# First block's norms: the first norm among the first modulation parts, the residual sum ahead of other vector work, first chunks of h marked singly

## What is computed

```python
def modulate(x, gain, shift, scale):
    return rms_norm(x, gain) * (1.0 + scale[:, None]) + shift[:, None]
def swiglu(h, w1, w3, w2):
    return (jax.nn.silu(h @ w1) * (h @ w3)) @ w2
    ...
    cond = jax.nn.silu(c)
    for l in range(DEPTH):
        mod = cond @ ada_w[l] + ada_b[l]
        sh1, sc1, g1, sh2, sc2, g2, sh3, sc3, g3 = jnp.split(mod, N_MOD, axis=-1)
        h = modulate(x, norm_ffn1[l], sh1, sc1)
        x = x + 0.5 * (1.0 + g1)[:, None] * swiglu(h, ffn1_w1[l], ffn1_w3[l], ffn1_w2[l])
        h = modulate(x, norm_mix[l], sh2, sc2)
        y = token_mix(h, ...)
        x = x + (1.0 + g2)[:, None] * y
        h = modulate(x, norm_ffn2[l], sh3, sc3)
        x = x + 0.5 * (1.0 + g3)[:, None] * swiglu(h, ffn2_w1[l], ffn2_w3[l], ffn2_w2[l])
```

## Time and profile before

| | us |
|---|---|
| median of 3 runs | 3086.55 |
| lowest, highest | 3086.18, 3090.66 |
| profiled execution, its own time | 3088.79 |
| its span in the trace | 3086.8 |
| TensorE busy | 2927.2 (95%) |
| VectorE busy | 2096.7 (68%) |
| ACT busy | 1469.9 (48%) |

### The profile page before, as it was taken

The page is one execution under the profiler, slowest core; times in us unless marked ns, Lnnn a source line. Parts: engine busy times, 40 slices in busy tenths (PEclk is TensorE's granted clock), DMA queues, the critical chain, the costliest instruction groups (busy, mean ns, idle before and its releaser), DMA issues.

```text
span 3086.8 us, 53817 instructions
## 1 busy us (share of the span) xinstructions
PE 2927.2 (95%) x22836; PEld 2616.9 (85%) x22836; DVE 2096.7 (68%) x3263; ACT 1469.9 (48%) x1965; POOL 148.2 (5%) x257
## 2 busy tenths in 40 slices
PE   5999999989989998999899999999999999999998
PEld 5888899878878887998788887889788988887887
DVE  5886757768868777566676467755676677556674
ACT  1545644545445364445354345544554345435552
POOL 1000000100000000002000022000100000004000
PEclk6999999999999999999999999999999999999999
DMA  7775326537758743364475533655365555452452
GB/s 248 231 250 162 123 75 208 184 123 241 240 190 264 238 151 99 97 205 151 139 234 167 158 100 110 191 177 164 106 196 184 170 168 183 143 179 83 137 187 99
DMA packets 524878, 521.41 MB, mean 169 GB/s; under 512 B 16615, under 2 KB 521904, under 8 KB 524640
## 3 DMA queue, kind: packets, MB, share of 16 engines
q1 hardware_dynamic: 522032, 517.28, 52.8%
q0 software_dynamic: 816, 0.27, 0.1%
q10 hardware_dynamic: 1792, 0.44, 0.1%
HBM read 516.90 MB, written 1.05 MB: 168 GB/s over the span
## 4 chain that ended last, share of the span: by engine, by line
PE 82%; DVE 9%; ACT 5%; issue 2%; DMA 1%; POOL 0%; SPq 0%; DVEq 0%; POOLq 0%; ACTq 0%
PE P L65 81%; DVE wsp L74 4%; ACT wsp L71 3%; ACT arena L71 1%; DVE ACC L82 1%; PE P L68 1%; DVE arena L74 1%; DVE arena L82 1%; ACT HX L71 1%; DMA raw<-in_ada_w 1%; DVE X L74 1%; ACT L71 0%; DVE HX L82 0%; DVE X L82 0%; DMA raw<-in_nsa_w_in 0%
## 5 line engine op out<-in xcount | busy, mean ns | idle before, releaser
L65 PE MATMUL P<-HX,wsp 128*128 128x512 f32 (+2 forms) x10688 | 1666.2, 318 | 29.8 <-DVE HX L82 18.4
L65 PEld LDWEIGHTS P<-HX,wsp 128*128 128x128 f32 (+1 forms) x10688 | 1505.3, 193 | 169.9 <-issue 21.0
L74 DVE TENSOR_TENSOR wsp<-raw,wsp 128x2048 fp32r<-128x2048 f32 (+3 forms) x448 | 964.6, 2155 | 393.8 <-ACT wsp L71 393.5
L71 ACT ACTIVATE wsp<-raw 128x2048 fp32r<-128x2048 f32 (+3 forms) x448 | 806.0, 1801 | 585.1 <-PE P L65 521.8
L65 PE MATMUL P<-FG,wsp 128*128 128x512 f32 (+1 forms) x2816 | 498.9, 338 | 1.4 <-DVE wsp L74 1.4
L65 PEld LDWEIGHTS P<-FG,wsp 128*128 128x128 f32 x2816 | 429.7, 188 | 65.7 <-DVE wsp L74 2.6
L71 ACT ACTIVATE arena<-P 128x512 f32<-128x512 f32 (+3 forms) x384 | 214.4, 568 | 558.0 <-PE P L65 557.2
L74 DVE TENSOR_TENSOR arena<-arena,P 128x512 f32<-128x512 f32 (+2 forms) x232 | 151.1, 652 | 203.2 <-ACT arena L71 169.7
L65 PE MATMUL P<-arena 64*64 64x64 f32 (+9 forms) x3936 | 244.7, 265 | 21.9 <-ACT arena L71 10.3
L65 PEld LDWEIGHTS P<-arena 64*64 64x64 f32 (+3 forms) x3936 | 195.2, 149 | 68.6 <-issue 33.8
L82 DVE SCALAR_TENSOR_TENSOR ACC<-raw,sm,ACC 128x256 f32<-128x256 f32 x476 | 230.8, 485 | 16.7
(11 more groups left out here) (110 smaller groups left out, 1437.4 us busy)
## 6 DMA issues: line engine op xcount, KB each, us to landing
raw<-in_ffn_w SPq DMA_DIRECT2D x120, 1024.0 KB, 5.3
raw<-in_ada_w SPq DMA_DIRECT2D x72, 1024.0 KB, 5.0
raw<-in_w_in SPq DMA_DIRECT2D x52, 1024.0 KB, 5.2
raw<-in_ffn_w_gate SPq DMA_DIRECT2D x44, 1024.0 KB, 5.3
raw<-in_ffn_w_up SPq DMA_DIRECT2D x44, 1024.0 KB, 5.3
raw<-in_ffn_w_down SPq DMA_DIRECT2D x32, 1024.0 KB, 5.0
raw<-in_ffn_w SPq DMA_DIRECT2D x16, 768.0 KB, 4.6
raw<-in_nsa_w_in SPq DMA_DIRECT2D x12, 1024.0 KB, 5.4
```

Source lines behind the costliest of these rows:

```text
L65: return self if self.e is None else self.e.matmul(*a, skip_group_check=True, **k)
L71: return self if self.e is None else self.e.activation(*a, **k)
L74: return self if self.e is None else self.e.tensor_tensor(*a)
```

## The change

1. Start. The squares, sums, root and reciprocal of norm 0 are moved ahead: on ACT behind the start's copies, on VectorE between the copies of X and its first part, on TensorE the sums stand behind part 0 and the spread behind part 1. `mod_dve` of a part now follows directly, and among the eight parts VectorE and ACT take no FFN weights; behind part 7 ACT splits two units and VectorE one (the low half of the gate weights). The second unit's low half, part 8 and a third unit stand behind the pass over h.
2. Constants. Of 1616 columns the first 256 are loaded first, the others after unit 11; their users wait for the new mark `more_in`.
3. TensorE's products of the parts, all 72, are made in pieces of 64 columns of weights, alternately to partitions 0 to 63 and 64 to 127 of the result, twice as many.
4. Tails of the FFNs and of the output product in the first block. The last additions to X go ahead of the split that stood in front of them, and where the next unit is a part, this part goes behind the pass over h (`ada=False`).
5. Marks. The first pair of chunks of h in the first block has a mark for each chunk (HT, hH and hL). The attention outputs, eight chunks, are waited for one by one in place of pairs.

```diff
         def ready_dve(e, u, last=None, ada=True):
             while made["dve"] <= (reached[u + 1] if last is None else min(last, reached[u + 1])):
                 x = made["dve"]
+                if units[x][3] == "ada" and not ada:
+                    return
...
@@ start_act
                 turned_act(e, t)
+            for q in range(4):
+                square_act(e, 0, q)
+            root_act(e, 0)
             ready_act(e, -1)
@@ start_dve
+            for q in (1, 2):
+                square_dve(e, 0, q)
+            root_dve(e, 0)
             ready_dve(e, -1)
@@ ada_pe
-                        ins = e.matmul(P[b][:, q:q + 1], w[:, k, 128 * q:128 * q + 128], COND[:, k:k + 1], start=k == 0, stop=k == 7)
+                        for x in range(2):
+                            ins = e.matmul(P[b][half(x), q:q + 1], w[:, k, 128 * q + 64 * x:128 * q + 64 * x + 64], COND[:, k:k + 1],
+                                           start=k == 0, stop=k == 7)
...
-                    ins = e.matmul(P[b][:, q:q + 1], ACC[j % 2][:, 128 * q:128 * q + 128], one, start=True, stop=True)
+                    for x in range(2):
+                        ins = e.matmul(P[b][half(x), q:q + 1], ACC[j % 2][:, 128 * q + 64 * x:128 * q + 64 * x + 64], one,
+                                       start=True, stop=True)
@@ norm_act
                         for c in (2 * q, 2 * q + 1):
+                            e.wait_ge(*HT_.at((n, q) if c else (n, 0, 0)))
                             ins = e.activation(hH[:, c, :], HT[:, c, :], ACT.Identity, bias=shift_of(n, c))
+                            if c == 0:
+                                ins.then_inc(*HHI.up((n, q, c)))
@@ h_pairs, att_pairs
-            return [HLO.at((n, q)) for q in range(4)]
+            return [HLO.at((n, q // 2) if q or n > 5 else (n, 0, 0)) for q in range(8)]
...
-            return [ALO.at((a, 2 * q + 1)) for q in range(4)]
+            return [ALO.at((a, q)) for q in range(8)]
@@ ffn_dve
-                if i < 11:
+                if i < 9 or i < 11 and n > 4:
                     ready_dve(e, u)
                     fill_dve(e, u)
+                elif i < 11:
+                    if i == 9:
+                        ready_dve(e, u, ada=False)
+                    fill_dve(e, u, True)
+                elif n < 5:
+                    ready_dve(e, U["f2", f][10], ada=False)
@@ resid_dve
-                if i < 3:
+                if i < 2 or i == 2 and coef is None:
                     ready_dve(e, u)
+                if i == 3 and coef is not None:
+                    ready_dve(e, U[key][2], ada=False)
@@ sync_program
-            e.dma_start(C[:, :], cst).then_inc(*c_in.up("c", 16))
+            e.dma_start(C[:, 0:256], cst[:, 0:256]).then_inc(*c_in.up("c", 16))
...
+                if u == 11:
+                    e.dma_start(C[:, 256:NCONST], cst[:, 256:NCONST]).then_inc(*more_in.up("c", 16))
@@ tensor_program
-            fill_pe(e, -1)
+            for j in range(8):
+                ada_pe(e, j)
+                if j == 0:
+                    sums_pe(e, 0)
+                if j == 1:
+                    spread_pe(e, 0)
@@ scalar_program
-            fill_act(e, -1)
             u = behind(-1)
+            ready_act(e, u, U["f3", 0][0])
@@ vector_program
-            fill_dve(e, -1)
             u = behind(-1)
+            for j in range(8):
+                mod_dve(e, j)
+                ready_dve(e, U["ada"][j], U["f1", 0][0] if j == 7 else U["ada"][7])
```

More of the change, by code:

```diff
@@ L156, in ar @@
             return v
+        more_in = count("more_constants_landed")
         c_in, x_in, pos_in = count("const_landed"), count("x_landed"), count("pos_landed")
@@ L338, in build, with ready_act @@
         made = {}
-        def ready_act(e, u):
-            while made["act"] <= reached[u + 1]:
+        def ready_act(e, u, last=None):
+            while made["act"] <= (reached[u + 1] if last is None else min(last, reached[u + 1])):
                 x = made["act"]
@@ L353, in ready_act, with ready_dve @@
                     ins.then_inc(*HI.up(x))
-        def ready_dve(e, u):
-            while made["dve"] <= reached[u + 1]:
+        def ready_dve(e, u, last=None, ada=True):
+            while made["dve"] <= (reached[u + 1] if last is None else min(last, reached[u + 1])):
                 x = made["dve"]
+                if units[x][3] == "ada" and not ada:
+                    return
                 made["dve"] += 1
@@ L444, in lin_wide @@
                     if pairs and m == 0:
-                        e.wait_ge(*pairs[kk // 2])
+                        e.wait_ge(*mark(pairs, kk))
                     s = slice(m * 128, m * 128 + 128)
@@ L456, in lins @@
                     between()
-                e.wait_ge(*pairs[q])
                 for kk in (2 * q, 2 * q + 1):
+                    e.wait_ge(*mark(pairs, kk))
                     for u, p in zip(us, ps):
@@ L630, in rope_dve @@
             e.wait_ge(*RVEC.at(0))
-            e.wait_ge(*c_in.at("c"))
+            e.wait_ge(*more_in.at("c"))
             e.tensor_scalar(RA, RA, C[:, C_FREQ:C_FREQ + 1], None, ALU.mult).then_inc(*RVEC.up(1))
@@ L809, in norm_act @@
         def norm_act(e, n, u):
-            if n == 0:
-                for q in range(4):
-                    square_act(e, 0, q)
             if late(n):
                 ready_act(e, u)
-            root_act(e, n)
+            if n:
+                root_act(e, n)
             if late(n):
@@ L819, in norm_act @@
                 for q in range(4):
-                    e.wait_ge(*HT_.at((n, q)))
+                    e.wait_ge(*HT_.at((n, q) if q or n > 5 else (n, q, 0)))
                     if n < 6:
@@ L830, in norm_dve @@
         def norm_dve(e, n, u):
-            if n == 0:
-                for q in (1, 2):
-                    square_dve(e, 0, q)
             if late(n):
                 ready_dve(e, u)
-            root_dve(e, n)
+            if n:
+                root_dve(e, n)
             if not late(n):
@@ L847, in norm_dve @@
                             ins = e.scalar_tensor_tensor(HT[:, c, :], X[:, c, :], scale_of(n, c), P[b][:, 0:256], ALU.mult, ALU.mult)
+                            if c == 0:
+                                ins.then_inc(*HT_.up((n, q, c)))
                         ins.then_inc(*HT_.up((n, q)))
@@ L850, in norm_dve @@
                         s = slice(2 * q - 2, 2 * q)
-                        e.wait_ge(*HHI.at((n, q - 1)))
                         if n < 6:
                             for c in (2 * q - 2, 2 * q - 1):
+                                e.wait_ge(*HHI.at((n, q - 1) if c else (n, 0, 0)))
                                 ins = e.scalar_tensor_tensor(hL[:, c, :], HT[:, c, :], shift_of(n, c), hH[:, c, :].bitcast(F32),
                                                              ALU.add, ALU.subtract)
+                                if c == 0:
+                                    ins.then_inc(*HLO.up((n, 0, 0)))
                         else:
+                            e.wait_ge(*HHI.at((n, q - 1)))
                             ins = e.tensor_tensor(hL[:, s, :], HT[:, s, :], hH[:, s, :].bitcast(F32), ALU.subtract)
@@ L861, in h_pairs, with mark @@
         def h_pairs(n):
-            return [HLO.at((n, q)) for q in range(4)]
+            return [HLO.at((n, q // 2) if q or n > 5 else (n, 0, 0)) for q in range(8)]
+        def mark(pairs, kk):
+            return pairs[kk if len(pairs) == 8 else kk // 2]
         AT = [ar(4608 + 512 * i, 512) for i in range(2)]
@@ L2647, in tensor_program @@
             start_pe(e)
-            fill_pe(e, -1)
+            for j in range(8):
[4 more added lines that the diff above has]
+                    spread_pe(e, 0)
             for l in range(2):
-                sums_pe(e, 3 * l)
-                spread_pe(e, 3 * l)
+                if l:
+                    sums_pe(e, 3)
+                    spread_pe(e, 3)
                 ffn_pe(e, 2 * l, 3 * l)
```

## The result

The changed kernel takes 3065.12 us (median of 4 runs, 3062.82 to 3071.72), the kernel before 3088.61 in the same comparison: a ratio of 0.9926, interval 0.9906 to 0.9946, some 23 us faster. In a second series, with the experiments, it takes 3060.26 against 3089.0 (0.9906, 0.9886 to 0.9927). The forecast was 3054.9 with a range of 3046 to 3065, so the sign was right, but the gain, 23.5 and 28.7 us by the two series, is 8 and 3 us smaller than the 31.7 forecast, and the first median stands just outside the range. The profiled execution is the slowest of its four, 3071.72 us, with a span of 3069.8.

What follows compares the result with a forecast made beforehand. TensorE was taken to bound the kernel, 82% of the chain. The terms 10.6 + 16.2 + 2.4 + 2.5 = 31.7 us took 3088.79 to 3057.1, and the median 2.2 below to 3054.9, range 3046 to 3065.

Steps and rivals of the forecast that it cites:

- What bounds the kernel: Whole kernel: TensorE is 82% of the chain, so time counts where it stands idle or its own instructions get shorter.
- The start, 10.6: Start: norm first and shorter parts bring the dense start to 56.2 from 66.76, 10.6 us gained, bounds 7 to 13.
- Rival B: Start: landings slip or the hold on part 1 is passed on, first product at 60, total 3059 us; chance 0.2.
- Norms 2, 3 and 5, 16.2: Tails before the norms: adding the result first gains 6.8 us at norm 3, 4.6 at 2 and 5, 16.2 together.
- the single marks, 2.4: First chunks of h one by one: 0.6 us at norms 2, 3 and 5, 0.3 at 1 and 4, together 2.4.
- Rival E: Norms 2, 3 and 5: additions stay behind something else on VectorE, 4 us gained in place of 16, 3067; chance 0.05.
- rival C: FFNs after norms 2, 3 and 5: VectorE's put-off work comes back, 9 to 10 us return, 3064; chance 0.1.
- The parts in the stream: 64 later parts between dense products: 0.33 us each with 64 columns in place of 0.37, 2.5 us gained, ends 0 and 5.
- The prediction's own sign of being wrong: Dense start later than 60, TensorE waiting for `wsp` after norms 2, 3 or 5, or dearer parts in the stream.
- The term's lower end: Parts in the stream: a gain of 0 us, with 0.37 us for a part if half is fixed cost.
- The clock, "no gain": First products after norms 2, 3 and 5: the clock falls in the shorter gaps too, so no gain was counted.
- Rival A: Norms 2, 3 and 5: the clock holds through the shorter gaps, 1.4 us each, 4.2 together, 3051; chance 0.08.

Runs made afterwards that it cites:

- the four kernels: Old or changed order at the start, each with 128- or 64-column pieces there: dense start at 66.8 and 61.3 (old), 63.1 and 55.5 us (changed).
- the tails: The changed kernel with the tails of the FFNs and the output product as before: 3072.79 us, ratio 0.996.
- the pairs: The changed kernel with the first pair of chunks of h marked and waited for as a pair again: 3068.47 us, ratio 0.9934.
- the old order: The kernel before with only the parts changed, all 72 in pieces of 64 columns: 3084.54 us, ratio 0.9994.
- the mixture of four sorts: The changed kernel with later parts in turn of 64 columns, 64 made twice, 128, and 128 made twice: 3076.49 us.

## Why the prediction was right at the start and the norms, and wrong in the stream

- **What bounds the kernel: right.** TensorE is 83% of the chain, and each gap that got shorter moved the end.
- **The start, 10.6: right, 11.3 seen.** The way there held too, landing by landing: part 7 at 39.3 as foreseen, the first gate weights at 42.3 for 42.6. That the shorter pieces and the new order need each other was said of one place only (the wait for the reciprocal); the four kernels show it for the whole. Rival B, a start at 60, did not come.
- **Norms 2, 3 and 5, 16.2, and the single marks, 2.4: right, 5.4, 7.8 and 5.3 seen in the gaps** where 5.2, 7.4 and 5.2 were foreseen for both together, and 1.0 in place of 0.4 at norms 1 and 4. Taken back alone the tails cost 12.5 us. Rival E is out by the additions' row, rival C by the 3 us that part and split ended ahead of TensorE's products, with 2.6 foreseen; TensorE waits for no `wsp` behind these norms.
- **The parts in the stream: this step failed.** The prediction took 0.33 us for a part, 0.04 less than before, 2.5 us gained in all with ends of 0 and 5. The stretch 174.38 - 174.01, from the part's first record to the next product, was taken for the cost of a part, and for 64 columns the same reading gives 0.33 (914.49 to 914.82), just as foreseen. But a price that lies ahead of the first record, or in the products around, is not in it. The interval from part to part, which holds everything, shows +0.07 in the best case, and +0.3 where the dense products run slower. The medians put 6.4 us lost (with intervals that overlap) in place of the 2.5 gained, a difference of 8.9; and the FFN stages of the change lose 6.5 to 9.4 us more than those of the kernels with 128 columns there. That is the whole miss in the gain of the first series, 8.2 us, and more than that of the second, 3.0. The prediction's own sign of being wrong, parts in the stream that become dearer, came true. The term's lower end was wrong by arithmetic too: with half of the 0.57 fixed, eight records cost 0.285 + 8 x 0.018 = 0.43, not 0.37, a loss of 0.06 for each of 64 parts. The end had to be some 4 us below nothing, and with it the range would have reached 3069.
- **The rule of the Trainium skill weighed at that step** (TensorEngine Tiling (Array Packing), Key Properties: a change of the tiling mode drains the engine) spoke against the edit, and the edit lost, though no row shows the drain itself. The answer given to it, that the 0.57 us of 16 records holds the drain, was wrong: the part's own stretch got shorter by 0.03 while the interval got longer by 0.07, so at least 0.1 us more lies outside of that stretch, where the weight loader is idle ahead of it. From interval to interval a part costs 0.45 us with 128 columns and 0.53 with 64, and not 0.37 and 0.33.
- **The clock, "no gain": right in direction, still too kind.** The first products behind the gap take 13.82, 13.81 and 12.84 us at norms 2, 3 and 5, before 13.15, 12.90 and 13.11; at norms 1 and 4 0.3 and 0.7 more. Together 2.4 us lost, where nothing was counted. The granted clock over the 7 us from the first product on goes with it: 0.61, 0.64 and 0.77, before 0.72, 0.76 and 0.72. But it is not the shorter gap alone: the kernel with 128 columns in the stream has gaps of 6.5 to 6.6 us there, and 13.20, 13.16 and 13.11 at clocks of 0.74 to 0.75. Rival A, a clock that holds, is out.
- **The sum with what was measured:** 31.8 in start and gaps, less 2.4 of the clock, less the 6.4 that taking back the pieces in the stream gave, is 23.0; the medians have 23.5 and 28.7. The traces, up to the second block, have 20.4 and 25.0; what they differ by between themselves is scatter of the mixers and of the rate in the FFNs, for which the prediction had no term. That start and gaps gave 2.6 us more than foreseen and the clock took 2.4 that was not foreseen is luck: the two cancel.

**What stays open.** The dense products of the FFN have two rates at the same granted clock of 1.00: 64 of them in 11.35 or in 11.58 us. All executions with 128 columns show mostly the faster one in the FFN of norm 3 (ten intervals 160.5 to 161.4, a single one at the slower rate among them here and there), all with 64 columns alone the slower (164.24 in both of the change, and in the kernels of the tails, the pairs and the old order). But the FFN of norm 2 in the first execution of the change was at the faster one (161.26), in the second at the slower (164.23), the kernel before has a place in its first FFN with 64 products in 11.54 us, and the mixture of four sorts ran fast behind each sort in the FFN of norm 3 and not in that of norm 2. An added load of 128 columns did not bring it back. And behind the last part of all, in the FFN of norm 5, where TensorE makes 384 products with no part among them, both rates come again, at a clock of 1.00. The rows are the first and the second execution of the change and the kernel with 128 columns in the stream:

```profile
1557.23 68.11 PE L65 MATMUL P<-HX,wsp 128*128 128x512 f32 x384
...
1554.76 66.83 PE L65 MATMUL P<-HX,wsp 128*128 128x512 f32 x384
...
1544.51 68.09 PE L65 MATMUL P<-HX,wsp 128*128 128x512 f32 x384
```

So the rate can last over hundreds of products, the same kernel has one or the other in the same place from one execution to the next, and pieces of 128 columns don't rule out the slower one. What sets it is not settled; that pieces of 64 columns in the stream mostly go with the slower one is all that the runs show.

## What to carry to other kernels

Read what a short instruction costs in a dense stream from interval to interval between its neighbours of the same kind, not from the gap between its own row and the next: here the one said -0.04 us and the other +0.07 to +0.3 us. Use narrow pieces of weights where TensorE is alone and limited by its own loads, as at a start at the low clock, and wide ones inside a stream of wide products; a switch has a price for each visit, and few instructions can't pay it. And after a wait is shortened, look at what is released last next: the same start gave 5.8 us more once the weights that it then waited for were split ahead of most of h and the bank in the way was taken later.

## What the runs showed of the chip

- At the 1.2 GHz level, a whole part made by TensorE took 6.97 us in 32 records of 128 columns of weights, and 3.58 in 64 records of 64 columns sent in turn to the two halves of the output: twice the records in half the time. Both are from traces with a granted clock of 0.50 from 20 to 40 us, the kernel before and the old order with 64 columns; the first trace of the change has clock records only from 60 us on, and the same 3.58.
- In the stream at 2.4 GHz a visit of such pieces cost some 0.38 us whatever its number, with the weight loader idle for 0.25 us ahead of it, and 17 ns for each further record, against 135 ns for one of 128 columns.
- The same products run at two rates, 11.35 and 11.58 us for 64 and 66.8 and 68.1 for 384, with the granted clock at 1.00 for both.
- A gap of 6.3 us in place of 14.1 did not keep the clock. Granted clocks by stretch of the changed kernel (us, busy of each engine, clock, DMA share, GB/s): 

```profile
874.00:881.00 7.00, 6.67 (x25) 5.73 (x26) 6.67 (x17) 4.25 (x7) 0.00 (x0) 0.61 0.27 93
881.00:888.00 7.00, 7.00 (x41) 5.92 (x39) 3.70 (x5) 0.53 (x2) 0.00 (x0) 1.00 0.61 192
```

The first 7 us behind the gap have 0.61, which is some 5.5 us at the 1.2 GHz level and the rest at 2.4, and the next 7 us are at 2.4 GHz.
